# Latent attention of a two-block decoder: queries on partitions and one pass over the logits in place of keys on partitions and two

## The reference

```python
def _attend(qb, qpos, k, v, kpos):
    scale = qb.shape[-1] ** -0.5
    s = jnp.einsum('bqhd,bkhd->bhqk', qb, k).astype(jnp.float32) * scale
    mask = kpos[None, :] <= qpos[:, None]
    s = jnp.where(mask[None, None], s, NEG_INF)
    p = jax.nn.softmax(s, axis=-1).astype(v.dtype)
    return jnp.einsum('bhqk,bkhd->bqhd', p, v)
...
    out_meta = _attend(q[:, :N_META], pos[:N_META], k[:, :N_META], v[:, :N_META], pos[:N_META])
...
    out_r = lax.map(lambda a: _attend(a[0], a[1], k, v, pos), (qr, pr))
```

## Time and profile before

| | |
|---|---|
| median of 3 runs | 2530.76 us (2528.82 to 2531.76) |
| the profiled execution | 2532.15 us |
| its span in the profile | 2530.4 us |
| TensorE busy | 2409.5 us, 95% of the span |
| VectorE, ScalarE, GpSimd busy | 825.6, 728.3 and 682.3 us |
| first logits of the attention, start | 1071.57 us |
| first matmul of `evout`, start | 1181.60 us |

### The profile page before, as it was taken

The page is one execution under the profiler, slowest core; times in us unless marked ns, Lnnn a source line. Parts: engine busy times, 40 slices in busy tenths (PEclk is TensorE's granted clock), DMA queues, the critical chain, the costliest instruction groups (busy, mean ns, idle before and its releaser), DMA issues.

```text
span 2530.4 us, 29422 instructions
## 1 busy us (share of the span) xinstructions
PE 2409.5 (95%) x11644; PEld 1719.2 (68%) x11644; DVE 825.6 (33%) x1286; ACT 728.3 (29%) x1089; POOL 682.3 (27%) x366
## 2 busy tenths in 40 slices
PE   7999999969999899989999999999999999999998
PEld 5585445743333348756899999988876477877875
DVE  2654312341111233341372063153000333721722
ACT  3324433311111311453322121243322334221222
POOL 3140012511111001210153343424432033544441
PEclk9699999979999999999999999999999999999999
DMA  4131111637999422200132222222222022322220
GB/s 150 61 98 52 52 34 45 265 124 284 359 358 380 188 67 88 67 9 26 50 101 84 88 90 81 96 88 92 91 75 67 0 75 67 100 89 95 92 87 37
DMA packets 68315, 275.41 MB, mean 109 GB/s; under 512 B 12488, under 2 KB 12616, under 8 KB 55920
## 3 DMA queue, kind: packets, MB, share of 16 engines
q1 hardware_dynamic: 59408, 259.61, 29.0%
q0 software_dynamic: 8512, 13.89, 1.6%
q10 hardware_dynamic: 288, 0.40, 0.1%
HBM read 321.02 MB, written 16.80 MB: 134 GB/s over the span
## 4 chain that ended last, share of the span: by engine, by line
PE 89%; issue 4%; DVE 3%; POOL 2%; ACT 2%; DMA 0%; DVEq 0%; POOLq 0%; SPq 0%; ACTq 0%
PE ps L816 16%; PE ps L803 14%; PE ps L1236 7%; PE ps L789 6%; PE ps L1006 4%; PE ps L1051 3%; PE ps L490 3%; PE ps L1258 3%; PE ps L1111 2%; PE ps L1197 2%; PE ps L701 2%; PE ps L1033 2%; POOL weights_low L2456 2%; PE ps L621 2%; PE ps L501 2%
## 5 line engine op out<-in xcount | busy, mean ns | idle before, releaser
L2456 POOL TENSOR_TENSOR weights_low<-weights,parts 128x1024 fp32r<-128x1024 f32 x218 | 547.9, 2516 | 1017.4 <-ACT parts L1728 1017.4
L816 PE MATMUL ps<-parts 128*128 128x512 f32 x1344 | 423.8, 395 | 9.2 <-DVE parts L1987 6.7
L803 PE MATMUL ps<-parts 128*128 128x264 f32 x2240 | 411.2, 285 | 8.1 <-DVE parts L1987 6.9
L1728 ACT ACTIVATE parts<-weights 128x1024 fp32r<-128x1024 f32 x218 | 229.1, 1055 | 443.7 <-PE ps L803 144.9
L803 PEld LDWEIGHTS ps<-parts 128*128 128x128 f32 x2240 | 349.5, 190 | 8.7 <-issue 8.7
L803 PE MATMUL ps<-parts,weights_low 128*128 128x264 f32 x1120 | 319.3, 285 | 0.0
L816 PEld LDWEIGHTS ps<-parts 128*128 128x128 f32 x1344 | 254.1, 189 | 70.8 <-issue 10.4
L816 PE MATMUL ps<-parts,weights_low 128*128 128x512 f32 x672 | 266.8, 397 | 0.0
L803 PEld LDWEIGHTS ps<-parts,weights_low 128*128 128x128 f32 x1120 | 213.2, 190 | 0.0
L1236 PE MATMUL ps<-area,normed 128*64 128x512 f32 x752 | 172.8, 601 | 1.6 <-DVE normed L2174 1.6
L1987 DVE TENSOR_TENSOR parts<-normed,parts 128x528 f32 (+1 forms) x64 | 155.0, 2421 | 9.6 <-DVE normed L1986 1.8
(11 more groups left out here) (419 smaller groups left out, 3327.3 us busy)
## 6 DMA issues: line engine op xcount, KB each, us to landing
weights<-in_weights SPq DMA_DIRECT2D x283, 512.0 KB, 3.4
area<-in_experts SPq DMA_DIRECT2D x141, 1024.0 KB
area<-pair_rows SPq DMA_DIRECT2D x4, 1024.0 KB, 8.2
residual<-in_x SPq DMA_DIRECT2D x4, 512.0 KB, 6.5
area<-bias_scratch POOLq DMA_DIRECT2D x1, 2048.0 KB, 9.7
token_rows<-area SPq DMA_DIRECT2D x1, 2048.0 KB, 6.6
out_tiles<-residual SPq DMA_DIRECT2D x4, 512.0 KB, 2.9
area<-in_decay POOLq DMA_DIRECT2D x2, 528.0 KB, 3.9
```

Source lines behind the costliest of these rows:

```text
L803: ins = mm(ps[:, b + h, 0:HALF], wt[:, k], x[:, m * DT + k, HALF * h:HALF * h + HALF], start=m == k == j == 0, stop=m == chunks - 1 and k ...
L816: ins = mm(ps[:, b], wt[:, k], x[:, m * DT + k, META:T2], start=m == k == j == 0, stop=m == chunks - 1 and k == DT - 1 and j == 2)
L1728: fn(high_slot(n, place), RING[:, n % SLOTS], ACT.Copy).then_inc(S["w_hi"], 1)
L2456: g.tensor_tensor(RING_LOW[:, n % SLOTS], RING[:, n % SLOTS], high_slot(n, place), ALU.subtract).then_inc(S["w_lo"], 1)
```

## The change

One pass instead of two. A unit is a pair of heads and a query block t, 16 units in all. For unit u TensorE makes the logits of both heads with queries on partitions (`logits`), VectorE adds the mask, scales and takes the largest in one instruction per head, whose output in on-chip memory is kept (`largest`; its sign is turned, so it is a minimum), ScalarE takes exponential and sum (`exponentials`), VectorE takes the reciprocals and scales the even head, GpSimd the odd head. TensorE turns the probabilities (`transposed`), ScalarE copies them out of the accumulator (`copy`), and TensorE multiplies them with the values (`outputs`), the two heads in the two column halves. After a pair ScalarE copies the output (`mla_y`). The 16 meta queries of all heads are handled once, in small instructions between units. The values are made before the last two gate projections instead of inside the attention, and their chunk `uv` stands earlier in `CHUNKS`. The work of the recurrence on ScalarE (`act_lru`), VectorE and GpSimd is no longer done ahead of the second pass but a piece at a time between units. The columns and rows of ones, and two memsets on GpSimd, go.

The core of the diff, its added lines:

```diff
-          ("evin", 11), ("uq", 2), ("uk", 1), ("evgate", 2), ("rg", 1), ("uv", 1), ("evout", 8), ("up0", 32), ("down0", 32),
+          ("evin", 11), ("uq", 2), ("uk", 1), ("uv", 1), ("evgate", 2), ("rg", 1), ("evout", 8), ("up0", 32), ("down0", 32),
...
+        VO = area(30596, 5, HEADS * HD)
+        LGM = [area(4236, 2, N2), area(5820, 2, N2), area(28972, 2, N2)]
+        PTR, PTM = [area(21660 + 1024 * j, 2, SEQ) for j in range(2)], [area(23708 + 256 * j, 2, P) for j in range(2)]
...
                     narrow(wt, PKV.unsqueeze(1), [(n, 0)], n == 0)
+                wv = take()[:, 0:4].rearrange("p k c -> p (k c)")
+                b = [2 * bank(), 2 * bank()]
+                w.count("act_evac", 3)
+                for j, b in enumerate((b[0], b[0] + 1, b[1], b[1] + 1, 6)):
+                    c, width = TOK2[j]
+                    if j == 0:
+                        begun(mm(ps[0:width, b, 0:256], PKV[:, c:c + width], wv[:, 0:256], start=True, stop=True))
+                        ins = mm(ps[0:width, b, 256:512], PKV[:, c:c + width], wv[:, 256:512], start=True, stop=True)
+                    else:
+                        ins = mm(ps[0:width, b], PKV[:, c:c + width], wv, start=True, stop=True)
+                    ins.then_inc(S["tile_done"], 1)
+                linear2([take()], xk, DT, behind=5)
+                linear2([take()], xk, DT, behind=4)
                 wt = take()
                 for n in range(8):
                     if n < 4:
                         pe.wait_ge(S["lru_x"], w.next("lru_x"))
+                    narrow(wt, XC, [(n, n % 4)], n == 0, behind=3 if n == 0 else None)
                 pe_mla()
...
                 flat = ps[:, :, :].rearrange("p b c -> p (b c)")
+                units = [(i, t) for i in range(PAIRS) for t in range(1, 5)]
+                n = len(units)
                 pe.wait_ge(S["act_evac"], w.value("act_evac"))
                 pe.wait_ge(S["q_ready"], 1)
                 pe.wait_ge(S["k_ready"], 1)
...
+                def logits(u):
+                    i, t = units[u]
+                    c, keys = TOK2[t][0], TOK2[t][0] + P
+                    for e in range(2):
+                        if u:
+                            pe.wait_ge(S["mla_max"], 2 * u + e - 1)
+                        for lo, hi in ((0, min(keys, 512)), (512, keys)):
+                            if hi > lo:
+                                ins = mm(flat[:, 1024 * e + lo:1024 * e + hi], QT2[0:96, 2 * i + e, c:c + P],
+                                         KT2[0:96, 2 * i + e, lo:hi], start=True, stop=True)
+                        ins.then_inc(S["mla_s"], 1)
+                def transposed(u):
+                    i, t = units[u]
+                    if u:
+                        pe.wait_ge(S["mla_pt"], u)
+                    pe.wait_ge(S["mla_even"], u + 1)
+                    pe.wait_ge(S["mla_odd"], u + 1)
+                    for e in range(2):
+                        mm(ps[0:META, 6, P * e:P * e + P], LGM[u % 3][:, e, 0:META], IDENT, is_transpose=True, start=True, stop=True)
+                        for k in range(t):
+                            ins = mm(ps[:, 4 + e, P * k:P * k + P], LGM[u % 3][:, e, TOK2[1 + k][0]:TOK2[1 + k][0] + P], IDENT,
+                                     is_transpose=True, start=True, stop=True)
+                    ins.then_inc(S["mla_t"], 1)
+                def outputs(u):
+                    i, t = units[u]
+                    pe.wait_ge(S["mla_pt"], u + 1)
+                    if t == 1 and i:
+                        pe.wait_ge(S["mla_y"], i)
+                    for j in range(t + 1):
+                        for e in range(2):
+                            h, kw = 2 * i + e, TOK2[j][1]
+                            x = PTR[u % 2][:, e, P * (j - 1):P * j] if j else PTM[u % 2][0:META, e]
+                            ins = mm(ps[HD * e:HD * e + HD, 7, P * (t - 1):P * t], VO[0:kw, j, HD * h:HD * h + HD], x,
+                                     start=j == 0, stop=j == t)
+                    if t == 4:
+                        ins.then_inc(S["mla_o"], 1)
...
+                logits(0)
+                logits(1)
+                meta_logits()
+                for u in range(n):
+                    if u in (1, 5, 9):
+                        pe.wait_ge(S[{1: "meta_max", 5: "meta_pt", 9: "mla_ym"}[u]], 1)
+                    if u + 2 < n:
+                        logits(u + 2)
+                    transposed(u)
+                    if u:
+                        outputs(u - 1)
+                    if u == 4:
+                        meta_transposed()
+                    if u == 8:
+                        meta_outputs()
+                outputs(n - 1)
             def values(i):
...
+                def exponentials(u):
+                    keys, st = TOK2[units[u][1]][0] + P, SMALL[:, 8 * (u % 3):8 * (u % 3) + 8]
+                    for e in range(2):
+                        act.wait_ge(S["mla_max"], 2 * u + e + 1)
+                        x = LGM[u % 3][:, e, 0:keys]
+                        fn(x, x, ACT.Exp, scale=-1.0, bias=st[:, e:e + 1], accum_out=st[:, 2 + e:3 + e]).then_inc(S["mla_p"], 1)
+                def copy(u):
+                    keys = P * units[u][1]
+                    act.wait_ge(S["mla_t"], u + 1)
+                    fn(PTM[u % 2][0:META], ps[0:META, 6, 0:2 * P].rearrange("p (e c) -> p e c", e=2), ACT.Copy)
+                    fn(PTR[u % 2][:, :, 0:keys], ps[:, 4:6, 0:keys], ACT.Copy).then_inc(S["mla_pt"], 1)
+                def outputs(i):
+                    act.wait_ge(S["mla_o"], i + 1)
+                    act.wait_ge(S["gelu_done"], i + 1)
+                    fn(Y2[:, 4 + i, META:], ps[:, 7], ACT.Copy).then_inc(S["mla_y"], 1)
...
+                lru_rates(0)
                 exponentials(0)
+                for u in range(n):
+                    if u + 1 < n:
+                        exponentials(u + 1)
+                    if u < 3:
+                        lru_rates(u + 1)
+                    if u == 2:
+                        act.wait_ge(S["act_ops"], w.next("act_ops", 4))
+                        nc.scalar.preload_act_table_set("natural_log_exp_and_others")
+                    if u == 1:
+                        meta_exponentials()
+                    if 3 <= u < 7:
+                        lru_inverse(u - 3)
+                    copy(u)
+                    if u == 4:
+                        meta_copy()
+                    if u == 8:
+                        meta_outputs()
+                    if u == 9:
+                        lru_roots()
+                    if u and u % 4 == 0:
+                        outputs(u // 4 - 1)
+                outputs(PAIRS - 1)
...
+                units = [(i, t) for i in range(PAIRS) for t in range(1, 5)]
+                n = len(units)
+                def largest(u):
+                    keys = TOK2[units[u][1]][0] + P
+                    if u >= 3:
+                        dve.wait_ge(S["mla_t"], u - 2)
+                    for e in range(2):
+                        dve.wait_ge(S["mla_s"], 2 * u + e + 1)
+                        settle()
+                        v.tensor_tensor_reduce(out=LGM[u % 3][:, e, 0:keys], in0=flat[:, 1024 * e:1024 * e + keys],
+                                               in1=MASKW[:, T2 - keys:T2], scale=-MLA_SCALE, scalar=-TAKEN, op0=ALU.add, op1=ALU.min,
+                                               accum_out=SMALL[:, 8 * (u % 3) + e:8 * (u % 3) + e + 1]).then_inc(S["mla_max"], 1)
+                def scale(u):
+                    keys, st = TOK2[units[u][1]][0] + P, SMALL[:, 8 * (u % 3):8 * (u % 3) + 8]
+                    dve.wait_ge(S["mla_p"], 2 * u + 2)
+                    v.reciprocal(st[:, 4:6], st[:, 2:4]).then_inc(S["mla_inv"], 1)
+                    dve.wait_ge(S["mla_inv"], u + 1)
+                    x = LGM[u % 3][:, 0, 0:keys]
+                    v.tensor_scalar(x, x, st[:, 4:5], None, ALU.mult).then_inc(S["mla_even"], 1)
...
+                largest(0)
+                largest(1)
+                for u in range(n):
+                    if u + 2 < n:
+                        largest(u + 2)
+                    if u == 0:
+                        meta_largest()
+                    scale(u)
+                    if u == 2:
+                        meta_scale()
+                    if 4 <= u < 8:
+                        root(u - 4)
+                    if u >= 11 and u < 15:
+                        recurrence(u - 11)
...
+                for u in range(4 * PAIRS):
+                    x = LGM[u % 3][:, 1, 0:TOK2[1 + u % 4][0] + P]
+                    pool.wait_ge(S["mla_inv"], u + 1)
+                    g.tensor_scalar(x, x, SMALL[:, 8 * (u % 3) + 5:8 * (u % 3) + 6], None, ALU.mult).then_inc(S["mla_odd"], 1)
+                    if u < 4:
+                        gelu_out(u)
```

(36 more changed lines are left out.)

255 lines of the change are left out of this document (72 added, 183 removed).

## The result

| | before | after |
|---|---|---|
| median | 2530.88 us (2528.82 to 2531.76) | 2551.62 us (2550.74 to 2556.97) |
| span in the profile | 2530.4 us | 2550.0 us |
| first logits of the attention | 1071.57 us | 1076.07 us |
| first matmul of `evout` | 1181.60 us | 1202.85 us |
| the attention | 110.0 us | 126.8 us |

The ratio is 1.0087, 95% interval 1.0075 to 1.0099: slower by 0.9%, where 0.5% faster was forecast. The whole difference lies at the place that the prediction looked at. The attention takes 16.8 us more and starts 4.5 us later, and what follows it takes 1347.15 us where it took 1348.80: 16.75 + 4.50 - 1.65 = 19.6 us, the difference of the spans.

What follows compares the result with a forecast made beforehand. TensorE, busy 2409.5 of 2530.4 us, was taken as the bound. New attention 80 + values 4.6 + bank wait 1.2 - old attention 110.0 = -24.2 us; clock +12 gave -12: 2519 us, range 2504 to 2534.

Steps and rivals of the forecast that it cites:

- the clock, +12 us: TensorE in the attention: clock partly down, +12 us chosen between 0 (full clock) and +37 (half clock throughout).
- rival 4: Slower: TensorE's clock falls in the start's wait and never returns, as 96-row matmuls with gaps do not restore it; 2544 us, chance 0.12.
- GpSimd's scaling, 0.27 to 0.63 us: Odd head's scaling in each round: 0.63 us for 528 keys, 0.27 estimated for 144, ending 0.1 to 0.25 us after VectorE.
- Rival 3: Little gain: clock mostly down or gaps longer, as GpSimd and VectorE wait for each other, +7 us; chance 0.13.
- The sum of the rest: Whole attention at full clock: start 6.6, four pairs 70.1, meta work 3.1, roots 2.1, edges -2.3; 80 us used.
- The matmuls: TensorE's attention work at full clock: logits 18.8, transposes 12.2, outputs 13.6, meta queries 3.1; 47.7 us in sum.
- The start: From the attention's start to the first transpose, with three units of logits, meta logits and a wait for ScalarE: 6.6 us.
- the meta queries: Small work in rounds 4 and 8, with a wait of 0.55 us each: 3.1 us.
- ScalarE's roots: Round 9: ScalarE loads the Sqrt table, takes four roots and loads back, some 4.9 us, of which 2.1 not hidden.
- the signs that would make the prediction wrong: Clock 1.00 or 0.50 throughout, gaps of 2.5 us, or `evout` waiting for `mla_y` or `lru_done`.
- outputs of both heads side by side: TensorE's output matmuls: the two heads run at once, 0.213 us a block, 13.6 us for four pairs.
- the values' wait for banks: Values, made before the last gate projections: 4.6 us of matmuls, plus 1.2 us waiting for one more copy.

Runs made afterwards that it cites:

- experiment 1: Also written `x_both`: the changed kernel with VectorE scaling the odd head too, and GpSimd scaling nothing; 2543.54 us, ratio 1.0046 to before.
- experiment 6: The changed kernel with both heads scaled on VectorE and three added 256-column matmuls a round before the wait for the scaling; 2508.79 us, ratio 0.9912.
- experiment 4: The changed kernel with four added 256-column matmuls a round on TensorE, before the wait for the scaling; 2521.33 us, ratio 0.9964 to before.
- x_fill2: The changed kernel with two added 256-column matmuls a round on TensorE, before the wait for the scaling; 2525.69 us, one run.
- x_scf: The changed kernel with `scale(u)` moved ahead of `largest(u+2)` on VectorE; 2508.74 us, ratio 0.9909 to before.

## Why the prediction was wrong

**The step that failed is the clock, +12 us.** It chose a third of the 37 us between full and half clock, because the busy share of 0.60 "lies nearer to the first pass than to idleness". With the gaps nearly as forecast (experiment 1) the stretch takes 118.5 us, and with the clock held up (experiment 6) 84.8: the clock costs 33.7 us, not 12. The busy share did not tell it: in experiment 1 TensorE is busy for 92.02 of 118.49 us, 0.78, a little more than the first pass's 0.76, and the clock is 0.57 where it was 1.00.

That is rival 4: 117 us and 2544 forecast for half clock throughout, 118.5 and 2543.5 measured in experiment 1. That its number fits so closely is in part luck, since it was worked out from matmuls priced too low, at a clock of 0.50 and not 0.57. It had been given a chance of 0.12. Against it stood that the clock was back 6.87 us behind the small matmuls; and the first pass, from which the third was taken, has gaps of up to 0.95 us, so it said nothing of gaps twice as long. Nor did the 27.1 us at 0.50, which were put down to 64-row matmuls: there the gaps are 0.20 to 0.44 us, and what kept the clock down in them is not tested. The rival's mechanism was half right. The clock fell behind the first long gap (2.61 us up to 1082.93) and stayed down but for short times. But the rows of the matmuls are not what kept it there: the same 96-row logits ran at 1.00 in experiments 4 and 6.

**GpSimd's scaling, 0.27 to 0.63 us**, was the second error. It was priced from the earlier trace rows, an instruction that multiplies and adds with two constants in another tile. This one takes 0.65 to 1.60 us alone and on average 1.06 to 2.17 beside VectorE, and a constant in place of the scalar saves only 0.07. So 13 of the 15 gaps were 2.30 to 3.35 us (the others 1.79 and 0.91) and not 1.4 to 1.75. Rival 3 had the contention at +7 us, but as a wait for VectorE alone.

**The sum of the rest was nearly right**, 80 us forecast and 84.8 measured with the clock at 1.00, but in part by errors that cancel. The matmuls were priced too low. One pair in experiment 6, start to start: logits 5.6 us (4.7 predicted), transposes 3.4 (3.05), outputs 4.2 (3.4): 13.3 where 11.15 were summed, so 8.6 us over four pairs, and the gaps were 0.1 us longer each. The start was as forecast, 6.5 us for 6.6. The rest took 5 us less than was put down for it: the meta queries take 0.71 and 0.97 us in rounds 4 and 8, where 3.1 were summed, and the longest wait in the rounds with ScalarE's roots is 1.14 us where others are 0.32, and 2.1 were put down. The remaining 2.5 us are not taken apart.

80 + 4.8 + 33.7 + 8.3 = 126.8 us, the stretch as measured; the forecast was 92. The last two terms depend on the order in which they are taken. Clock first, with GpSimd still at work, is experiment 4: 126.8 - 97.1 = 29.7 us, and then 12.3 for GpSimd. So the clock costs 30 to 34 us and GpSimd's price 8 to 12, less where the clock is down anyway.

**Right** were the outputs of both heads side by side (about 0.22 us a block more, at full clock); the values' wait for banks (TensorE waits 1.43 us, 1.2 forecast); that what follows the stretch hardly changes (1.65 us less); that ScalarE does not bound (53.96 us of work); that `evout` waits for neither `mla_y` nor `lru_done`. The later start, 4.5 us where 5.8 were forecast, fits, but says little: in the thirteen profiles of changed kernels, whose TensorE programs are the same up to there, the attention starts anywhere from 1073.64 to 1077.68 us. Round 9 shows no longer wait than the others (2.31 us), since nearly every gap was already as long. Of the signs that would make the prediction wrong, it had named both that came: a clock near 0.50 and gaps of 2.5 us.

**The transposes.** The rule of the Trainium skill ("TensorE: Matmul & The Clock Gate", Part 4: PE-mode transpose), cited in the prediction, that a transpose does not count as busy in the same way, was set beside the time nearest to the measured one, 2544 us. The runs do not bear it out as the cause: with the same 112 transposes the clock is 1.00 in experiments 4 and 6, and what differs is the idle time. Whether a transpose counts for less than a matmul no run separates, since both experiments add matmuls.

## What to carry to other kernels

Where a change replaces solid matmuls by a chain through several engines, price it at both clocks and do not give half clock a small chance unless other work fills the gaps: here the same chain took 118.5 us, or 84.8 with 48 added matmuls in its gaps that held the clock up. Ask of each wait whether the waiting instruction's inputs were ready before the instruction that stands ahead of it in its queue: moving `scale(u)` ahead of `largest(u + 2)`, one line, was worth 43 us. Where an operation is priced from a row of another instruction, the same engine, name and shape are not enough: give its price a range, and say what it does to the chain at the upper end.

## What the runs showed of the hardware that was not expected

- 27 us of added matmuls made the kernel 30 us faster (2551.6 to 2521.3), and 16 fewer of them, with both heads on VectorE, 43 us (to 2508.8).
- GpSimd's multiply by a scalar per partition takes 0.65, 0.96, 1.28 and 1.60 us at 144, 272, 400 and 528 float32 columns, and by one constant 0.07 us less; the recurrence's multiply and add with two constants takes 0.63 at 528. Beside VectorE's own multiply 0.10 to 0.30 us come on top, and 0.63 to 0.84 where VectorE goes straight on to the recurrence.
- Behind gaps of 1.49 and 1.75 us in turn, after two of 2.29 and 2.81, TensorE ran at 0.50 for most of 118 us (`x_both`); with gaps of 1.29 to 1.81 us and 0.85 us more work a round it held 1.00 for the first 38 us (`x_fill2`); and behind a single one of 1.70 us, after 10 us of nearly unbroken work, it fell (`x_scf`). That a single gap's length does not decide is shown; what does was not taken apart.
